# Eight-expert mixer kernel: the products of the experts' ranks with 128 rows made as two products of 64 weight columns each

## What is computed

```python
def swiglu(t, wg, wu, wd):
    return (jax.nn.silu(t @ wg) * (t @ wu)) @ wd

def moe_swiglu(h, router_w, wg, wu, wd):
    t = h.reshape(bsz * s, d)                       # 512 tokens x 1024
    logits = (t @ router_w).astype(jnp.float32)
    top_logits, top_idx = lax.top_k(logits, TOP_K)  # 2 of 8 experts
    top_w = jax.nn.softmax(top_logits, axis=-1)
    gates = jnp.einsum('tk,tke->te', top_w, jax.nn.one_hot(top_idx, N_EXPERTS, ...))
    for e in range(N_EXPERTS):
        y = y + gates[:, e:e + 1] * swiglu(t, wg[e], wu[e], wd[e])
```

## Time and profile before

| what | value |
|---|---|
| median of 3 runs | 1998.9 us (1997.22 to 2002.45) |
| profiled execution, first to last instruction (span) | 1994.0 us |
| the program's own time in that execution | not listed apart from its span |
| granted TensorE clock over the span | 0.994 |
| TensorE matmul busy | 1956.1 us, 98% |
| TensorE weight loads busy | 1657.7 us, 83% |
| VectorE, ScalarE, GpSimd busy | 43%, 29%, 34% |

### The profile page before, as it was taken

How to read it: one execution, slowest core, us unless ns; L and a number is a source line. 1 busy time by engine, 2 the same in 40 slices (tenths; PEclk the granted TensorE clock), 3 DMA queues, 4 the chain that set the end, 5 groups by cost and what they waited for, 6 DMA issues and landing times. The chain is left out here.

```text
span 1994.0 us, 28678 instructions
## 1 busy us (share of the span) xinstructions
PE 1956.1 (98%) x11076; PEld 1657.7 (83%) x11076; DVE 864.3 (43%) x1177; ACT 568.5 (29%) x1210; POOL 677.9 (34%) x582
## 2 busy tenths in 40 slices
PE   8999998999999999999999999999999999999997
PEld 7778644888647888888869999756999999999996
DVE  4898597666515444444257667532100000000023
ACT  1443113555412111110055466522121111111102
POOL 5756331656224434345337766511200000000011
PEclk9999998999999999999999999999999999999999
DMA  8214741222125556522121111102956568678893
GB/s 328 82 53 168 282 144 32 91 85 89 55 86 199 205 198 209 188 88 98 61 84 65 44 63 64 54 11 88 329 192 236 200 222 289 229 257 298 318 343 144
DMA packets 82710, 312.66 MB, mean 157 GB/s; under 512 B 10136, under 2 KB 10656, under 8 KB 82448
## 3 DMA queue, kind: packets, MB, share of 16 engines
q1 hardware_dynamic: 75952, 289.73, 41.2%
q0 software_dynamic: 4320, 13.76, 2.0%
q10 hardware_dynamic: 2304, 7.33, 1.0%
HBM read 301.43 MB, written 9.36 MB: 156 GB/s over the span
## 5 line engine op out<-in xcount | busy, mean ns | idle before, releaser
L3100 PE MATMUL banks<-sb_act,sb_ring 128*128 128x192 f32 (+3 forms) x3696 | 500.9, 298 | 2.4 <-issue 2.4
L3100 PEld LDWEIGHTS banks<-sb_act,sb_ring 128*128 128x128 f32 x3696 | 498.6, 191 | 3.1 <-issue 2.7
L287 PE MATMUL banks<-sb_x_norm,sb_ring 128*128 128x256 f32 x1224 | 288.4, 380 | 2.0 <-ACT sb_ring L451 2.0
L287 PEld LDWEIGHTS banks<-sb_x_norm,sb_ring 128*128 128x128 f32 x1224 | 230.3, 190 | 37.2 <-issue 6.6
L3424 DVE TENSOR_TENSOR sb_act<-sb_work,banks 128x128 f32<-128x128 f32 (+3 forms) x88 | 27.7, 315 | 510.8 <-PE banks L3100 493.6
L426 POOL TENSOR_TENSOR sb_ring<-sb_ring 128x512 f32<-128x512 f32 x146 | 207.4, 1420 | 105.8 <-PE banks L287 47.1
L2959 POOL DMA_INDIRECT sb_work<-first_expert_rows,sb_table x8 | 7.5, 936 | 461.0 <-DMA first_expert_rows<-sb_x_norm 458.8
L287 PE MATMUL banks<-sb_work,sb_ring 128*128 128x256 f32 x640 | 150.6, 380 | 1.0 <-ACT sb_ring L451 1.0
L287 PEld LDWEIGHTS banks<-sb_work,sb_ring 128*128 128x128 f32 x640 | 120.2, 190 | 16.8 <-issue 1.2
L3226 ACT ACTIVATE sb_work<-banks 128x128 f32<-128x128 f32 (+3 forms) x88 | 26.2, 299 | 311.2 <-PE banks L3100 306.1
L1513 PE MATMUL banks<-sb_act,sb_ring 128*128 128x512 f32 x256 | 112.4, 594 | 0.0
(11 more groups left out here) (518 smaller groups left out, 3009.1 us busy)
## 6 DMA issues: line engine op xcount, KB each, us to landing
sb_ring<-in_w_moe_up SPq DMA_DIRECT2D x176, 512.0 KB
sb_ring<-in_w_moe_down SPq DMA_DIRECT2D x64, 704.0 KB
sb_act<-in_cond_w SPq DMA_DIRECT2D x84, 512.0 KB, 3.8
sb_ring<-in_w_ffn_up SPq DMA_DIRECT2D x44, 512.0 KB
sb_ring<-in_w_h_in SPq DMA_DIRECT2D x32, 512.0 KB
sb_ring<-in_w_in SPq DMA_DIRECT2D x28, 512.0 KB
sb_ring<-in_w_m_in SPq DMA_DIRECT2D x24, 512.0 KB
sb_ring<-in_w_ffn_down SPq DMA_DIRECT2D x16, 704.0 KB
```

The lines of the kernel that those rows point to most:

```text
L287: last = m.nc.tensor.matmul(out, lhs(k), rhs(k), start=(k == 0 and not onto), stop=(k == n - 1), skip_group_check=onto)
L3100: last = nc.tensor.matmul(ps[:, b % BANKS, 0:cap], w, act, start=(k == 0), stop=(k == kt - 1))
```

## The change

Where a rank has 128 rows or fewer (ranks 5, 6 and 7, up and down blocks), each product is made as two: the first takes columns 0 to 63 of the stationary operand and writes PSUM partitions 0 to 63, the second takes columns 64 to 127 and writes partitions 64 to 127. Both stream the same moving operand. Ranks 0 to 4 keep the product of 128 columns.

```diff
@@ -3097,8 +3097,9 @@
                                                                 hid[:, k, 0:cap])
                             if b >= up and r >= turned_ranks:
                                 w, act = act, w
-                            last = nc.tensor.matmul(ps[:, b % BANKS, 0:cap], w, act, start=(k == 0),
-                                                    stop=(k == kt - 1))
+                            for c in ([slice(0, P)] if cap > P else [rows(i, P // 2) for i in range(2)]):
+                                last = nc.tensor.matmul(ps[c, b % BANKS, 0:cap], w[:, c], act, start=(k == 0),
+                                                        stop=(k == kt - 1))
                         last.then_inc(m.blocks_done, 1)
```

## The result

The changed kernel takes 2005.97 us (median of 6 runs, 2003.81 to 2008.28) beside 1997.91 us for the kernel before (6 runs, 1996.80 to 2002.45). The ratio is 1.0036 with a 95% interval of 1.0025 to 1.0047. That is 7 us slower by the ratio, 8 by the two medians: inside the range given (1995 to 2008), but 5.5 us above the likeliest time of 2000.5 and just outside "within 0.3%", the case that was held likeliest (the interval of the ratio takes in both sides of that line). One traced execution of a later version took 2280 us at a granted clock of 0.844 and is left out of every comparison. The profiled execution took 2006.4 us, with a span of 2004.4 us against 1994.0.

What follows compares the result with a forecast made beforehand. TensorE was taken as the bound (matmuls busy 98%), so only record spacing could win time. Steps -3.7 us and switches +5.35 us gave +1.65 us on 1998.9, likeliest 2000.5 us, range 1995 to 2008.

Steps and rivals of the forecast that it cites:

- within 0.3%: Whole kernel: time indistinguishable from the kernel before, 0.3% being about 6 us; chance 79%.
- The step: Ranks 5 to 7, 1584 products: start-to-start time from 111.7 to 109.2 ns, -4.0 us, of which -3.7 us counts.
- rival C: Halved products: accumulation or shared moving operand removes the step gain, switches stand alone, 2004.3 us; chance 12%.
- D (not what it says): Halved products: compiler merges or reorders the halves, time as before, 1998.9 us; chance 3%.
- The switches: Ranks 5 to 7: leaving and re-entering halves costs 0.295 us per transpose detour, 0.35 per 512-column product; +5.35 us in all.
- Rival B: Ranks 5 to 7: switches hidden by loads pulled ahead, only the step's gain left, 1995.2 us; chance 7%.
- Ranks 5 and 6: Net of steps and switches there: rank 5 0.7 us shorter, rank 6 1.1 us shorter.
- is only waited for: Rank 7 before 1924.5: step gain of 128 steps lost in TensorE's dry stretch, 0.3 us.
- The sum of +1.65 us: Whole kernel: step gain of -3.7 us plus switches of +5.35 us, giving 2000.5 us.
- dearer switches: Ranks 5 to 7: upper price of the switches, 20 entries and exits at 0.35 us, 7 us.
- rival A: Halved products: instructions come too slowly, 2181 us at worst; chance 13% of a shortfall costing over 4 us.

Runs made afterwards that it cites:

- X and Z: Two of three chips used for follow-up runs; the unaltered changed kernel against the kernel before: ratio 1.0025 on the first, 1.0029 on the second.
- chip Y: Third follow-up chip, versions against the kernel before: only ranks 5 and 6 in halves 0.9996; rank 7's down blocks whole 0.9990, up blocks whole 1.0016; 512-column product halved too 0.9992.

## Why the prediction was right and where it failed

**The step: right in size.** 111.7 to 109.2 ns in accumulating blocks, with one moving operand for both halves, for 38 us on end. That the 2.5 ns are the load of 128 columns ending last was read off and the earlier trace rows; no run separates it from another cost of a 128-column product. Loads of 64 columns take 137 ns as in the earlier trace rows. The prediction's rivals C (no gain) and D (not what it says) are out.

**The switches: right, in number and price.** Each of the four delays stands in the changed trace, and a full turn of a down block with both kinds of detour got 0.6 us longer (4.35 beside 3.75), where the steps and switches of the prediction give 0.295 + 0.35 - 22 x 0.0025 = 0.59. Rival B (hidden) is out. The price of a detour is 0.3 to 0.35 us there and back. The Trainium skill says "Mode switching requires drain" (TensorEngine Tiling (Array Packing), Tiling Modes). By that rule a detour can't be free, and the trace agrees.

**Ranks 5 and 6: right** (-0.75 and -1.0 against -0.7 and -1.1), and too small for any of these measurements to tell from nothing.

**The failing step** is the sentence "In rank 7 TensorE runs dry between 1921 and 1924.5 with the DMA at 393 GB/s and fully busy: weight blocks and GpSimd's gathers share it", and the one behind it, that what is won ahead of it "is only waited for". I took the dry stretch for a wait for weight blocks, which does not depend on how many instructions a block has. It is a stop inside a block while GpSimd issues its gathers, and the same stop begins 4.4 us earlier when every product is two. That it is a shortage of instructions is the reading that fits all of this. The term stood at +0.3 us (gain lost); on chips of the kind of X and Z it is 9.2 - 4.6 = +4.6 us. With the gain of all steps, -0.9 us in these blocks, they come to +3.7 where the sum had -0.6. The sum of +1.65 us so becomes about +5.9, beside ratios of 1.0036, 1.0025 and 1.0029, which are 7.2, 5.0 and 5.8 us. On chip Y the first sum seems to hold: the version with the 512-column product in halves has 0.9992 there, which is -1.6 us, and 2.4 us for that product brings it to +0.8, with an interval of 2 us each way. The changed kernel itself was not run there.

**Luck.** That 2006 us fell inside the range is in part luck. Its upper end was set by rival C (no gain in the step) and dearer switches, which did not come, and by a mild rival A over the whole length; the loss came from one stop that no term of the sum had.

**Rival A was the right kind of thing in the wrong place.** It let four instructions per step be too many for the whole of 177 us, at a chance of 13% and with nothing between a mild and a ruinous price. In the steady run the supply has no trouble: 27 ns an instruction for 38 us. The Trainium skill's 62 ns per MATMUL with microcode decoding (TensorE: Matmul & The Clock Gate, section "Wait — 56ns, not 53.3ns?") would, as an estimate, give two matmuls 124 ns; the trace has 109.2 ns, so it does not bind here. What A should have asked is where the supply is disturbed already, and the rows had it: a stop of TensorE at record 122 of blocks with 16 records, named "issue", next to GpSimd's gathers.

**How much of the loss is the clock** was not separated. The stretch at the 1.2 GHz level begins 2.6 to 4.1 us after the beginning of a stop, in both kernels, and on chip Y, where the stop is absent, there is none in rank 7. It lasts 6.8 to 10.2 us with halves and none, 3.4 or 6.8 us with whole products. In the changed kernel's first trace 4.8 us of full work at 0.50 cost 2.4 us. Two traces of the kernel before come nearest to a separation: with a stop of 3.5 us and no fall its up blocks are 3.3 us over full pace, with a stop of 2.3 us and a fall for 6.8 us they are 5.9 us over. So a fall cost some 3 us there, and what halves add in all their traces is above all the longer stop, 7.4 us beside 3.1 on average.

**Open:** why TensorE gets so few instructions while GpSimd issues its gathers, and why it does not stop on chip Y, where the same eight gathers are issued at the same distance of 1.24 us. Issuing the gathers further apart, or earlier, was not tried.

## What to carry to other kernels

Two products of 64 stationary columns side by side beat one of 128 by 2.5 ns in 112 here, and every detour to another tile shape costs 0.3 us; it takes some 120 steps in one stretch to earn one detour. Before instructions are doubled, look at each idle stretch of TensorE whether it stops at a block's end or inside a block: a stop inside, named "issue", is no wait for weights, and here it began 4.4 us earlier and lasted more than twice as long with doubled instructions. Don't take a long time between instruction packets for the cause before you have counted what was used up between them. The version with halves in ranks 5 and 6 alone is the only one that came out below the kernel before on two chips (0.9996 and 0.9994), and no measurement here proves it faster.

## What the runs showed that was not expected

- TensorE can all but stop inside a block while eight indirect gathers of GpSimd (0.5 MB each) are issued, with one or a few instructions every 0.7 us. It was so on two chips of three and in the first runs, in the kernel before as well, from record 122 to 133 of rank 7 with whole products and from record 183 to 198 with halves. The beginning is tied to the first gather (3.3 us after it with halves, 7.7 with whole products), the end to the last.
- It is not so everywhere: on chip Y no trace of the same program has this stop, and weight blocks were late by 0.6 us instead.
- The granted clock fell to the 1.2 GHz level within each of the four stops of 7.3 to 7.5 us. In the kernel before, it fell at a stop of 2.3 us in one trace and not at one of 3.5 us in the other.
